# First kind of layer: the keys' squares summed ahead of scaling the queries, the differential outputs turned one group at a time, the gate's product kept apart from the powers

## The chip, the cores and the metric

The kernel runs on one core of one Trainium2 chip. The metric is the device time of one execution in microseconds. The engines are named as the profile has them: PE is TensorE (matmuls and transposes), PEld its weight loads, DVE is VectorE, ACT is ScalarE, POOL is GpSimd and SP is SyncE, which here only issues the loads of weights.

## The reference

The model has four layers on 256 rows of 1024 features: two of a first kind, then two of a second kind. The change touches only the first kind, and there only its mixing half:

```python
h = rms_norm(x, attn_norm_g[l])
rq, rk, rv, rg, dq, dk, dv = split(h @ w_in[l])            # 7 x 512 columns
ret = retention_bidir(rq, rk * 64 ** -0.5, rv, lg_f, lg_b) # 8 heads of 64
ret = rms_norm(ret, ret_norm_g[l]) * silu(rg)
dqn = rms_norm(dq, dq_norm_g[l]) * 64 ** -0.5              # 4 heads of 2 x 64
dkn = rms_norm(dk, dk_norm_g[l])
da  = diff_attention(dqn, dkn, dv, lam, slopes)            # 4 heads of 128
da  = rms_norm(da, diff_norm_g[l]) * (1 - lam_init)
x   = x + concatenate([ret, da]) @ w_out[l]
```

After that comes a gated feed-forward part (w_gate, w_up, w_down).

## The kernel before, in words

All matrix products of weights are float32 done in three passes. Weights are loaded by SyncE in slabs of 512 rows by 512 columns (128 partitions x 4 x 512) into a ring of four. ScalarE rounds a slab to its high half (`split_hi`, L1019), VectorE subtracts to get its low half (`split_lo`, L1512), and TensorE multiplies high by high, high by low and low by high (L492, L493, L494 for a whole slab, L509, L510, L511 for half of one). The splits run three slabs ahead of TensorE; a new load waits until the slab that lay in its place has been split.

Nothing is scheduled by a planner. Each engine has its own program, written out by hand in order, and waits on counting semaphores. The order within one engine's program is thus the order of its work, and a wait holds up all that is behind it on that engine.

A layer of the first kind projects `h` onto seven blocks of 512 columns: DQ, DK, DV, RQ, RK, RV, RG. While TensorE works on the later blocks, the attention of the earlier ones is put between its slabs by the generator `side()`. TensorE writes transposes and the heads' outputs into two turning banks, taken in turn. `turn_free` counts how many of them have been read out, so a piece of work can start only when the bank two before has been freed. `dve_ready` counts results of VectorE that are ready to be turned.

The steps that the change and the prediction touch are these.

* The scaled queries and keys of differential attention. ScalarE takes the projected block (`take_proj`, L1119) and squares it (`square_heads`, L1180). VectorE sums the squares over each head (`means`: the reduction is L1692, the mean L1561). GpSimd raises 16 columns to the power -0.5 (`root`, L2118), and VectorE multiplies (`norm_heads`, which calls `over_rms`, L1698). This is done for the queries (0) and for the keys (1). TensorE waits once for both, and turns the first two pairs of heads (`diff_pair`, transposes at L526).
* Retention. `ret_scores` (L632) makes the scores of a head, `retain` on VectorE (L1684) multiplies them by the decay, and `ret_values` (L649) makes the outputs of two heads in a turning bank. ScalarE copies these to `mixed1` (`take_outputs`, L1126) and squares a half of them, four heads, at a time (`square_outputs`, L1174). VectorE sums, GpSimd takes the power over 8 columns, and `ret_half` (L1698) multiplies the gated outputs by it.
* The gate. ScalarE takes the block RG through Silu (`take_proj(RG, 2, ACT.Silu)`, L1119, with a load of the activation table ahead of it). GpSimd multiplies the gate by the outputs, a half at a time (L2148).
* Turning `mixed1`. Eight tiles of 128 columns are turned in four groups of two: groups 2 and 3 are the differential outputs, 0 and 1 the retention outputs. ScalarE reads a turned group as its high half (`mixed_hi`, L1149) and VectorE as its low half (`mixed_lo`, L1541), which frees the bank. They are the left operands of w_out, whose four slabs are multiplied in half products of two tiles (`half_product`), so that TensorE can begin with the differential outputs while the retention outputs are still being made.

Before the change, `turn_mixed((2, 3))` (L665, called from `side()`) waits for `dve_ready` and turns both differential groups one behind the other, into both turning banks. ScalarE takes both high halves, then RG, then the outputs of heads 2 and 3. GpSimd does, for each half, the gate's product first (with a wait for its own result) and then the power. VectorE does a slab's split between each retention mean and the `ret_half` that belongs to it.

Of the kernel before, what the change touches and what calls it, by code (L numbers as in the profile page):

```python
# [24 lines left out]
ALU = mybir.AluOpType  # L25
# [113 lines left out]

STEPS_ACT1, STEPS_ACT2 = 4, 8  # L140
STEPS_DVE1, STEPS_DVE2 = 27, 86
STEPS_POOL1, STEPS_POOL2 = 2, 24
SMALL_LOADS = 5


# [39 lines left out]
def build(nc, t, out):  # L185
    with ExitStack() as ctx:
# [3 lines left out]
        def sem(name):  # L190
            return ctx.enter_context(nc.semaphore(name))
# [138 lines left out]
        decays_in = sem("decays_in")  # L330
        conv_in = sem("conv_in")
        outputs_in = sem("outputs_in")
        act_job = sem("act_job")
        conv_out = sem("conv_out")
        act_step = sem("act_step")
# [134 lines left out]
        def _(pe):  # L470
# [64 lines left out]
            def turn_model(src, groups, skip=0):  # L535

                for g in groups:
                    turn_group([(src[:, r, kt * P:(kt + 1) * P], (kt % 2) * SEQ + r * P)
                                for kt in (2 * g, 2 * g + 1) for r in range(R)], skip if g == groups[-1] else 0)
# [56 lines left out]
            for l in q.rounds(DEPTH, dict(slab=len(KTS1), blk=BLOCKS1, turn=TURNS1, scores=16, dve=9)):  # L596
# [62 lines left out]
                def ret_pair(j):  # L659
                    if j == 0:  # L660
                        read_out(projection[5])
                    group["ret", j] = turn_pair(lambda r: proj1[:, r, RQ + j * P:RQ + (j + 1) * P],
                                                lambda r: proj1[:, r, RK + j * P:RK + (j + 1) * P])

                def turn_mixed(groups):  # L665
                    pe.wait_ge(dve_ready, q.next("dve"))
                    turn_model(mixed1, groups)
                    return q.now("turn")

                def side():  # L670

                    pe.wait_ge(dve_ready, q.next("dve", 2))
                    diff_pair(0)
                    diff_pair(1)
                    yield
                    for h in range(DH):
                        diff_scores(h)
                        if h < 2:
                            diff_pair(h + 2)
                        else:  # L680
                            turn_combined(h - 2)
                        if h == 3:
                            diff_values(0)
                        yield
                    turn_combined(2)
                    diff_values(1)
                    ret_pair(0)
                    ret_pair(1)
                    yield
                    turn_combined(3)  # L690
                    diff_values(2)
                    ret_scores(0)
                    ret_scores(1)
                    yield
                    diff_values(3)
                    ret_values(0)
                    ret_scores(2)
                    ret_scores(3)
                    ret_pair(2)
                    yield  # L700
                    group["mixed"] = turn_mixed((2, 3))
                    ret_values(1)
                    ret_scores(4)
                    ret_scores(5)
                    ret_pair(3)
                    yield

# [10 lines left out]

                a = [open_block()]
                s = [take_slab()]  # L720
                pe.wait_ge(turn_free, group["mixed"] + 2)
                half_product(a[0], s[0], (0, 1), (0, 1), first=True)
                ret_values(2)
                ret_scores(6)
                ret_scores(7)
                turned_half = turn_mixed((0,))
                half_product(a[0], s[0], (2, 3), (2, 3)).then_inc(slab_used, 1)
                ret_values(3)
                s.append(take_slab())
# [2 lines left out]
                a.append(open_block())  # L732
                s.append(take_slab())
                half_product(a[1], s[2], (0, 1), (4, 5), first=True)
                turned_half = turn_mixed((1,))
                s.append(take_slab())
                half_product(a[1], s[3], (0, 1), (0, 1))
                pe.wait_ge(turn_free, turned_half + 2)
# [254 lines left out]
        def _(act):  # L993
# [110 lines left out]
            for l in q.rounds(DEPTH, per1):  # L1104
# [127 lines left out]
                decays((6, 7))  # L1232
                splits(1)
                mixed_hi(0, G_D)
                mixed_hi(2, G_D)
                take_proj(RG, 2, ACT.Silu)
                take_outputs(P)
                square_outputs(0, HALF)
                take_pair(3)
                splits(1)  # L1240
                take_outputs(2 * P)
# [253 lines left out]
        def _(dve):  # L1495
# [141 lines left out]
            loop4 = dict(slab=4, used=4, blk=2)  # L1637
            for l in q.rounds(DEPTH, dict(slab=len(KTS1), used=len(KTS1), blk=BLOCKS1, turn=TURNS1,
                                          turn_hi=4 + 4 + 11 + 4, squares=9, rstd=7, act_done=11, scores=16,
                                          decay=RH, probs=DH, step=STEPS_DVE1)):  # L1640
                ahead = iter(KTS1[AHEAD:] + KTS1[:AHEAD])

                def splits(n):
# [59 lines left out]
                def ret_half(c):  # L1703

                    root()
                    over_rms(mixed1[:, :, c * HALF:(c + 1) * HALF], proj1[:, :, RG + c * HALF:RG + (c + 1) * HALF],
                             S_OR + 8 * c, 4, HD).then_inc(dve_ready, 1)

# [23 lines left out]
                square_means(0)  # L1732
                splits(1)
                others(1)
                norm_heads(0)
                square_means(1)
                splits(1)
                norm_heads(1)
                splits(1)
# [20 lines left out]
                over_rms(v, v, S_PR, DH, DVD).then_inc(dve_ready, 1)  # L1760
                splits(1)
                mixed_lo(0, G_D)
                mixed_lo(2, G_D)
                others(2)
                q.next("turn", 3)
                retain((4, 5))
                means(S_O, sqo[:, :, 0:HALF], 4, HD)
                splits(1)
                ret_half(0)
                retain((6, 7))  # L1770
                mixed_lo(4, G_R)
                splits(1)
                q.next("turn")
                means(S_O + 8, sqo[:, :, HALF:NB], 4, HD)
                splits(1)
                ret_half(1)
                mixed_lo(6, G_R)
                added(0, l * 16 + 8)
                added(1, l * 16 + 8)
# [331 lines left out]
        def _(pool):  # L2111
# [17 lines left out]
            for l in q.rounds(DEPTH, dict(mean=7, outputs=2, decay=RH, blk=BLOCKS1, step=STEPS_POOL1)):  # L2129
                def diagonals(heads):  # L2130

                    for h in heads:
                        pool.wait_ge(decay_arg, q.next("decay"))
                        pool.tensor_tensor(decay[h][:, P:SEQ], decay[h][:, P:SEQ], decay[h][:, 3 * P:2 * SEQ],
                                           ALU.mult).then_inc(decay_ready, 1)

                root_x()
                root(stat[:, S_QR:S_QR + 16], stat[:, S_Q:S_Q + 16], 16)
                root(stat[:, S_QR + 16:S_QR + 32], stat[:, S_Q + 16:S_Q + 32], 16)
                diagonals(range(6))  # L2140
                root(stat[:, S_PR:S_PR + 8], stat[:, S_P:S_P + 8], 8)
                diagonals((6, 7))
                pool.wait_ge(acc_free, q.now("blk") + 7 + 2)
                for c in range(2):
                    pool.wait_ge(outputs_in, q.next("outputs"))
                    v = proj1[:, :, RG + c * HALF:RG + (c + 1) * HALF]
                    hold(pool)
                    step(pool.tensor_tensor(v, v, mixed1[:, :, c * HALF:(c + 1) * HALF], ALU.mult))  # L2148
                    at = 8 * c
                    root(stat[:, S_OR + at:S_OR + at + 8], stat[:, S_O + at:S_O + at + 8], 8)  # L2150
                root_x()
                q.next("blk", BLOCKS1)
            for l in q.rounds(DEPTH, dict(mean=4, blk=BLOCKS2, step=STEPS_POOL2)):
# [69 lines left out]
```

## Time and profile before

| | |
|---|---|
| runs | 1497.16, 1498.7 and 1499.43 us, median 1498.7 |
| the profiled execution: time, span | 1496.12 us, 1494.3 us |
| mean granted clock of TensorE | 0.995 of full speed |
| PE busy | 1446.4 us, 97% of the span |
| DVE busy | 942.6 us, 63% |
| ACT busy | 783.3 us, 52% |
| POOL busy | 105.1 us, 7% |
| split to the low half, L1512 | 251 instructions, 2187 ns mean |
| split to the high half, L1019 | 251 instructions, 1825 ns mean |
| power, L2118 | 23 instructions, 2475 ns mean |

The span runs from the first to the last instruction of the profiled execution; its time is 1.8 us more. The part of the span before about 322 us is layer one of the first kind, that from there to about 645 us is layer two, and the second kind follows. The granted clock is given as a share of TensorE's full 2.4 GHz. A matmul's end is modelled, and the starts are exact, so distances between starts are the better measure of TensorE.

### The profile page before, as it was taken

Reading aid. Unit: us, or ns where it says so; the run is one execution under the profiler, and the core shown is the slowest. Engines: PE = TensorE matmul, PEld = TensorE weight load, DVE = VectorE, ACT = ScalarE, POOL = GpSimd, SP = SyncE. Lnnn points to the kernel's source line nnn. Section 1 sums busy time; section 2 is a strip of 40 time slices with the busy share of each in tenths; the row PEclk is TensorE's granted clock in tenths of the full one; section 3 lists DMA queues with packets and bytes.
Section 4 is the critical chain, followed back from the end, with each engine's and each line's share of the span. In section 5 each row is a group of like instructions: output and inputs, shape, how many; then the busy total and the mean of one; then the engine's idle time right before and its main releaser. Section 6 shows DMA issues by size and latency. Waiting matters only on the chain.

```text
span 1494.3 us, 21705 instructions
## 1 busy us (share of the span) xinstructions
PE 1446.4 (97%) x7095; PEld 1203.2 (81%) x7095; DVE 942.6 (63%) x1120; ACT 783.3 (52%) x1012; POOL 105.1 (7%) x111
## 2 busy tenths in 40 slices
PE   5999999999999999999999999999999999999997
PEld 4787888888778888887888888888778888888885
DVE  5565655445755655445678878764456788787544
ACT  5574644345664444445666546544366765465442
POOL 0213000001212000000220000000002200000000
PEclk9999999999999999999999999999999999999998
DMA  7543555464433655555344566555553545666541
GB/s 278 194 140 115 172 194 193 144 205 163 154 128 111 228 190 175 169 198 179 114 164 148 190 225 197 179 192 192 172 180 113 177 151 175 224 197 196 190 149 43
DMA packets 174070, 257.74 MB, mean 172 GB/s; under 512 B 8765, under 2 KB 91919, under 8 KB 173839
## 3 DMA queue, kind: packets, MB, share of 16 engines
q1 hardware_dynamic: 170432, 249.95, 50.6%
q10 hardware_dynamic: 3535, 6.51, 1.4%
q8 instruction: 52, 0.85, 0.2%
q14 instruction: 51, 0.42, 0.1%
HBM read 255.39 MB, written 1.05 MB: 172 GB/s over the span
## 4 chain that ended last, share of the span: by engine, by line
PE 53%; issue 40%; POOL 3%; DVE 2%; ACT 1%; DMA 1%; ACTq 0%; DVEq 0%; POOLq 0%
PE bank L492 13%; PE bank L494 13%; PE bank L493 13%; PE bank L954 4%; PE bank L526 3%; POOL stat L2118 2%; PE bank L953 2%; PE bank L649 1%; PE bank L632 1%; PE bank L606 1%; DMA crows<-in_conv_rows 1%; PE bank L509 1%; PE bank L510 1%; PE bank L511 0%; PE bank L623 0%
## 5 line engine op out<-in xcount | busy, mean ns | idle before, releaser
L1512 DVE TENSOR_TENSOR w_lo<-w_raw,w_hi 128x2048 fp32r<-128x2048 f32 (+1 forms) x251 | 547.6, 2187 | 221.3 <-ACT w_hi L1019 218.5
L1019 ACT CAST w_hi<-w_raw 128x2048 fp32r<-128x2048 f32 (+1 forms) x251 | 455.9, 1825 | 226.1 <-PE bank L494 204.4
L492 PE MATMUL bank<-w_hi,hT 128*128 128x512 f32 (+1 forms) x1056 | 419.1, 397 | 7.7 <-DVE w_lo L1512 6.1
L494 PE MATMUL bank<-w_hi,hT 128*128 128x512 f32 (+1 forms) x1056 | 411.8, 390 | 0.0
L493 PE MATMUL bank<-w_lo,hT 128*128 128x512 f32 (+1 forms) x1056 | 411.1, 389 | 0.0
L492 PEld LDWEIGHTS bank<-w_hi,hT 128*128 128x128 f32 x1056 | 199.0, 188 | 48.4 <-DVE w_lo L1512 6.5
L494 PEld LDWEIGHTS bank<-w_hi,hT 128*128 128x128 f32 x1056 | 198.8, 188 | 41.5
L493 PEld LDWEIGHTS bank<-w_lo,hT 128*128 128x128 f32 x1056 | 199.2, 189 | 38.1
L954 PE MATMUL bank<-hT,w_hi 128*128 128x512 f32 x512 | 178.2, 396 | 0.4 <-DVE sum L2061 0.4
L2118 POOL TENSOR_TENSOR stat<-stat,cst 128x2 f32<-128x2 f32 (+3 forms) x23 | 56.9, 2475 | 1155.6 <-DVE stat L1561 1015.3
L953 PE MATMUL bank<-hT,w_lo 128*128 128x256 f32 x448 | 125.2, 279 | 0.0
L954 PEld LDWEIGHTS bank<-hT,w_hi 128*128 128x128 f32 x512 | 94.4, 188 | 21.4 <-issue 1.3
L492 PE MATMUL bank<-w_hi,hid2T_hi 128*128 128x512 f32 x256 | 99.8, 390 | 0.0
L494 PE MATMUL bank<-w_hi,hid2T_lo 128*128 128x512 f32 x256 | 99.7, 389 | 0.0
L493 PE MATMUL bank<-w_lo,hid2T_hi 128*128 128x512 f32 x256 | 99.6, 389 | 0.0
L953 PEld LDWEIGHTS bank<-hT,w_lo 128*128 128x128 f32 x448 | 84.4, 188 | 1.3
L492 PE MATMUL bank<-w_hi,hid1T_hi 128*128 128x512 f32 x176 | 69.1, 392 | 0.0
L494 PE MATMUL bank<-w_hi,hid1T_lo 128*128 128x512 f32 x176 | 68.6, 390 | 0.0
L493 PE MATMUL bank<-w_lo,hid1T_hi 128*128 128x512 f32 x176 | 68.5, 389 | 0.0
L1541 DVE SCALAR_TENSOR_TENSOR hT<-bank,gcols,hT 128x256 fp32r<-128x256 f32 (+1 forms) x76 | 34.2, 506 | 48.7 <-ACT hT L1049 41.4
L1042 ACT CAST hid1T_hi<-bank 128x512 f32 (+1 forms) x22 | 12.9, 586 | 90.3 <-PE bank L526 90.3
L1462 ACT COPY cross<-bank 128x256 f32<-128x256 f32 x64 | 20.8, 378 | 70.8 <-PE bank L954 70.8
(261 smaller groups left out, 1637.5 us busy)
## 6 DMA issues: line engine op xcount, KB each, us to landing
w_raw<-in_w_gate SPq DMA_DIRECT2D x108, 512.0 KB, 3.9
w_raw<-in_w_up SPq DMA_DIRECT2D x108, 512.0 KB, 4.5
w_raw<-in_w_down SPq DMA_DIRECT2D x104, 512.0 KB, 4.4
w_raw<-in_w_in SPq DMA_DIRECT2D x88, 512.0 KB, 4.3
w_raw<-in_w_out SPq DMA_DIRECT2D x16, 512.0 KB, 4.1
w_raw<-in_w_branch SPq DMA_DIRECT2D x32, 256.0 KB, 3.0
w_raw<-in_w_o SPq DMA_DIRECT2D x16, 512.0 KB, 4.6
bgate<-in_b_gate ACTq DMA_DIRECT2D x16, 256.0 KB, 3.3
```

What stands on the lines that cost most here:

```text
L492: pe.matmul(o, hi[:, kt, rows_of(r)], w_hi[:, s, j, 0:cols], start=begin, stop=False)
L493: pe.matmul(o, hi[:, kt, rows_of(r)], w_lo[:, s, j, 0:cols], start=False, stop=False)
L494: mm = pe.matmul(o, lo[:, kt, rows_of(r)], w_hi[:, s, j, 0:cols], start=False, stop=end)
L509: pe.matmul(a[r][:, :], hT_hi[:, kt, rows_of(r)], w_hi[:, s, j, :], start=begin, stop=False)
L526: tr = pe.transpose(b[0:m, col:col + n], src, ident[0:n, 0:n])
L953: pe.matmul(o[:, 0:SEQ], lo[:, kt, cols], hT_hi[:, kt, :], start=False, stop=False)
L954: mm = pe.matmul(o[:, :], hi[:, kt, cols], hT[:, :, kt, :], start=kt == 0, stop=kt == KT - 1)
L1019: act.copy(w_hi[:, s, 0:kts, :], w_raw[:, s, 0:kts, :]).then_inc(hi_ready, 1)
L1462: ins = act.copy(cross2[:, n, :], a[n][:, SEQ:2 * SEQ])
L1512: dve.tensor_tensor(w_lo[:, s, 0:kts, :], w_raw[:, s, 0:kts, :], w_hi[:, s, 0:kts, :].bitcast(F32), ALU.subtract).then_inc(lo_ready, 1)
L1541: return dve.scalar_tensor_tensor(lo, src, gain, hi.bitcast(F32), ALU.mult, ALU.subtract)
L2118: pool.tensor_tensor(dst, src, half[:, 0:n], ALU.pow).then_inc(rstd_ready, 1)
```

## The change

On TensorE the wait on `dve_ready` moves out of `turn_mixed`, which now turns one group. Group 2 is turned where both were, group 3 behind the values of heads 2 and 3 and the scores of heads 4 and 5, and the second half product of the first slab gets a wait for group 3.

On ScalarE the outputs of heads 2 and 3 are taken and squared ahead of RG, and the high half of group 3 is taken behind RG.

On VectorE the keys' squares are summed ahead of scaling the queries. The low half of group 3 moves behind the retention mean of the first four heads. In both halves of the retention outputs the slab's split moves from ahead of `ret_half` to behind it, and `ret_half` waits for a new semaphore, `gated`.

On GpSimd the gate's product signals `gated` instead of being waited for by GpSimd itself, and the order becomes power 0, product 0, product 1, power 1 where it was product 0, power 0, product 1, power 1.

```diff
@@ counts of self-waits, and the semaphore
-STEPS_POOL1, STEPS_POOL2 = 2, 24
+STEPS_POOL1, STEPS_POOL2 = 0, 24
+        gated = sem("gated")
@@ TensorE
-                def turn_mixed(groups):
-                    pe.wait_ge(dve_ready, q.next("dve"))
-                    turn_model(mixed1, groups)
+                def turn_mixed(g):
+                    turn_model(mixed1, (g,))
                     return q.now("turn")
...
-                    group["mixed"] = turn_mixed((2, 3))
+                    pe.wait_ge(dve_ready, q.next("dve"))
+                    group["mixed", 0] = turn_mixed(2)
                     ret_values(1)
                     ret_scores(4)
                     ret_scores(5)
+                    group["mixed", 1] = turn_mixed(3)
                     ret_pair(3)
...
-                pe.wait_ge(turn_free, group["mixed"] + 2)
+                pe.wait_ge(turn_free, group["mixed", 0] + 2)
                 half_product(a[0], s[0], (0, 1), (0, 1), first=True)
                 ret_values(2)
                 ret_scores(6)
                 ret_scores(7)
-                turned_half = turn_mixed((0,))
+                pe.wait_ge(dve_ready, q.next("dve"))
+                turned_half = turn_mixed(0)
+                pe.wait_ge(turn_free, group["mixed", 1] + 2)
                 half_product(a[0], s[0], (2, 3), (2, 3)).then_inc(slab_used, 1)
...
-                turned_half = turn_mixed((1,))
+                pe.wait_ge(dve_ready, q.next("dve"))
+                turned_half = turn_mixed(1)
@@ ScalarE
                 mixed_hi(0, G_D)
-                mixed_hi(2, G_D)
-                take_proj(RG, 2, ACT.Silu)
                 take_outputs(P)
                 square_outputs(0, HALF)
+                take_proj(RG, 2, ACT.Silu)
+                mixed_hi(2, G_D)
                 take_pair(3)
@@ VectorE
                 def ret_half(c):
 
                     root()
+                    dve.wait_ge(gated, q.next("gated"))
...
                 square_means(0)
                 splits(1)
                 others(1)
+                square_means(1)
                 norm_heads(0)
-                square_means(1)
                 splits(1)
                 norm_heads(1)
...
                 mixed_lo(0, G_D)
-                mixed_lo(2, G_D)
                 others(2)
-                q.next("turn", 3)
+                q.next("turn")
                 retain((4, 5))
                 means(S_O, sqo[:, :, 0:HALF], 4, HD)
-                splits(1)
+                mixed_lo(2, G_D)
+                q.next("turn", 2)
                 ret_half(0)
+                splits(1)
                 retain((6, 7))
                 mixed_lo(4, G_R)
                 splits(1)
                 q.next("turn")
                 means(S_O + 8, sqo[:, :, HALF:NB], 4, HD)
-                splits(1)
                 ret_half(1)
+                splits(1)
                 mixed_lo(6, G_R)
@@ GpSimd
-                pool.wait_ge(acc_free, q.now("blk") + 7 + 2)
-                for c in range(2):
+                def gate_half(c):
+                    v = proj1[:, :, RG + c * HALF:RG + (c + 1) * HALF]
                     pool.wait_ge(outputs_in, q.next("outputs"))
-                    v = proj1[:, :, RG + c * HALF:RG + (c + 1) * HALF]
                     hold(pool)
-                    step(pool.tensor_tensor(v, v, mixed1[:, :, c * HALF:(c + 1) * HALF], ALU.mult))
+                    pool.tensor_tensor(v, v, mixed1[:, :, c * HALF:(c + 1) * HALF], ALU.mult).then_inc(gated, 1)
+
+                def root_half(c):
                     at = 8 * c
                     root(stat[:, S_OR + at:S_OR + at + 8], stat[:, S_O + at:S_O + at + 8], 8)
+
+                root_half(0)
+                pool.wait_ge(acc_free, q.now("blk") + 7 + 2)
+                gate_half(0)
+                gate_half(1)
+                root_half(1)
```

## Rows read from the trace of the kernel before

**Rows 1.** Waits of TensorE over the span: total us, times, longest us.
```profile
PE bank L649 <- DVE hT L1541: 3.0, 2, 1.5
```

**Rows 2.** Timeline of TensorE, 55 to 59 us: start us, us, instruction, [idle before <-releaser].
```profile
55.38 0.39 PE L494 MATMUL bank<-w_hi,hT 128*128 128x512 f32 x1
57.37 1.09 PE L526 MATMUL bank<-cst,proj 128*128 128x128 f32 x8 [1.60 <-DVE proj L1698]
58.21 0.47 PE L492 MATMUL bank<-w_hi,hT 128*128 128x512 f32 x1
```

**Rows 3.** Timeline of VectorE, 49 to 58 us.
```profile
49.53 1.22 DVE L1692 TENSOR_REDUCE stat<-proj 128x16 f32<-128x1024 f32 x1
...
50.87 2.28 DVE L1512 TENSOR_TENSOR w_lo<-w_raw,w_hi 128x2048 fp32r<-128x2048 f32 x1
55.94 1.29 DVE L1698 TENSOR_TENSOR proj<-proj,stat 128x512 f32<-128x512 f32 x2 [2.79 <-POOL stat L2118]
```

**Rows 4.** Timeline of ScalarE, the keys' square.
```profile
46.22 1.06 ACT L1180 ACTIVATE proj<-proj 128x1024 f32<-128x1024 f32 x1
```

**Rows 5.** Timeline of GpSimd, 50 to 166 us.
```profile
51.03 4.87 POOL L2118 TENSOR_TENSOR stat<-stat,cst 128x16 f32<-128x16 f32 x1 [2.75 <-DVE stat L1561]
...
113.42 1.64 POOL L2118 TENSOR_TENSOR stat<-stat,cst 128x8 f32<-128x8 f32 x1 [26.09 <-DVE stat L1561]
...
124.27 1.28 POOL L2148 TENSOR_TENSOR proj<-proj,mixed 128x512 f32<-128x512 f32 x1 [7.29 <-ACTq L1173]
127.05 3.63 POOL L2118 TENSOR_TENSOR stat<-stat,cst 128x8 f32<-128x8 f32 x1 [1.50 <-DVE stat L1561]
...
162.74 2.70 POOL L2118 TENSOR_TENSOR stat<-stat,cst 128x2 f32<-128x2 f32 x1 [20.18 <-DVE stat L1561]
```

**Rows 6.** Timeline of VectorE, splits that ran beside powers.
```profile
126.90 2.29 DVE L1512 TENSOR_TENSOR w_lo<-w_raw,w_hi 128x2048 fp32r<-128x2048 f32 x1
...
162.59 4.49 DVE L1512 TENSOR_TENSOR w_lo<-w_raw,w_hi 128x2048 fp32r<-128x2048 f32 x2
```

**Rows 7.** Timeline of TensorE, layer one, 119 to 144 us.
```profile
119.04 1.03 PE L526 MATMUL bank<-cst,mixed 128*128 128x128 f32 x8
121.57 1.99 PE L649 MATMUL bank<-proj,ret_p 128*128 128x64 f32 x16 [1.50 <-DVE hT L1541]
123.49 1.14 PE L632 MATMUL bank<-qkT 64*128 64x256 f32 x8
124.57 0.66 PE L526 MATMUL bank<-cst,proj 128*128 128x128 f32 x4
...
127.83 1.89 PE L649 MATMUL bank<-proj,ret_p 128*128 128x64 f32 x16
...
131.53 0.66 PE L526 MATMUL bank<-cst,mixed 128*128 128x128 f32 x4 [0.74 <-DVE mixed L1698]
...
134.79 1.89 PE L649 MATMUL bank<-proj,ret_p 128*128 128x64 f32 x16
...
143.41 0.66 PE L526 MATMUL bank<-cst,mixed 128*128 128x128 f32 x4 [1.18 <-DVE mixed L1698]
```

**Rows 8.** Timeline of ScalarE, 119 to 125 us.
```profile
119.84 1.26 ACT L1149 ACTIVATE hT<-bank,gcols 128x512 fp32r<-128x512 f32 x2 [2.02 <-PE bank L526]
121.12 1.28 ACT L1119 ACT_TABLE_LOAD   x1
122.42 1.26 ACT L1119 ACTIVATE proj<-bank,stat 128x512 f32<-128x512 f32 x2
...
124.17 0.63 ACT L1174 ACTIVATE sqo<-mixed 128x512 f32<-128x512 f32 x1
```

**Rows 9.** Timeline of TensorE, layer two.
```profile
378.52 1.09 PE L526 MATMUL bank<-cst,proj 128*128 128x128 f32 x8 [1.59 <-DVE proj L1698]
...
465.30 0.66 PE L526 MATMUL bank<-cst,mixed 128*128 128x128 f32 x4 [1.18 <-DVE mixed L1698]
```

**Rows 10.** Busy us by window: PE, PEld, DVE, ACT, POOL, then granted clock, DMA.
```profile
445.00:446.00 1.00, 1.00 (x8) 0.65 (x4) 0.00 (x0) 0.81 (x2) 0.59 (x1) 0.50 0.02 7
```

More of the change, by code:

```diff
@@ L1639, in _ @@
                                           turn_hi=4 + 4 + 11 + 4, squares=9, rstd=7, act_done=11, scores=16,
-                                          decay=RH, probs=DH, step=STEPS_DVE1)):
+                                          decay=RH, probs=DH, gated=2, step=STEPS_DVE1)):
                 ahead = iter(KTS1[AHEAD:] + KTS1[:AHEAD])
@@ L1762, in _ @@
                 mixed_lo(0, G_D)
-                mixed_lo(2, G_D)
                 others(2)
-                q.next("turn", 3)
+                q.next("turn")
                 retain((4, 5))
                 means(S_O, sqo[:, :, 0:HALF], 4, HD)
+                mixed_lo(2, G_D)
+                q.next("turn", 2)
+                ret_half(0)
                 splits(1)
-                ret_half(0)
                 retain((6, 7))
@@ L1774, in _ @@
                 means(S_O + 8, sqo[:, :, HALF:NB], 4, HD)
+                ret_half(1)
                 splits(1)
-                ret_half(1)
                 mixed_lo(6, G_R)
```

## The prediction

> **What bounds the kernel now.** I read the page first: TensorE is busy for 97% of the span and no other engine for more than 63%, so only idle time of TensorE, or a lower clock on it, can be won back. Then the list of who TensorE waited for. Nearly all of its waits in the two layers of the first kind that this change touches are on VectorE, and they stand at four places, which the timeline of TensorE shows one by one. A: before the first diff pair is turned, 1.60 us for the scaled keys [rows 2]. B: before the retention values of heads 2 and 3, 1.50 us until a turning bank comes free, once in each layer, 3.0 us in all [rows 1, 7]. C: before the first pair of gated retention outputs is turned, 0.74 us. D: before the second pair, 1.18 us [rows 7]. In layer two A and D repeat (1.59 and 1.18) [rows 9], B repeats [rows 1], and C is missing, because TensorE arrived later there: its granted clock was 0.50 just behind B [rows 10], half of the 2.4 GHz that it has elsewhere. The distance from A to D is 86.04 us in layer one (57.37 to 143.41) and 86.78 in layer two (378.52 to 465.30) [rows 2, 7, 9], so that stretch cost 0.74 us net.
>
> Next I ask what makes VectorE late at A, C and D. It is each time GpSimd's power (L2118). Eight columns took 1.64 us at 113.42, but 3.63 us at 127.05, and the difference is VectorE's split of a slab (L1512), which ran from 126.90 to 129.19: the power ended 1.49 us behind it. Sixteen columns at 51.03 took 4.87 us and ended 2.75 us behind the split of 50.87. Two columns at 162.74 ended at 165.44, 0.56 us behind the first of two splits and in the middle of the second [rows 3, 5, 6]. So a power stands still while VectorE subtracts two SBUF tiles, and goes on when that one instruction ends; its own time is 1.64 us for 8 columns and about 2.8 for 16.
>
> **A: keys' squares ahead of scaling the queries.** ScalarE's square of the keys ends at 46.22 + 1.06 = 47.28 [rows 4]. VectorE reduces at 47.3 rather than at 49.53; the power can start 1.50 us behind the reduction (49.53 to 51.03) [rows 3, 5], at 48.8. The queries' scaling then runs on VectorE from 48.7 to 50.0 (1.29 us in two halves [rows 3]) and the split behind it to 52.2. Both read two SBUF tiles, so what the power does between them isn't shown by any row; the nearest is the two-column power, which was let in between two such instructions. I take that: in at 49.4, done at 52.1. The other end is a power held behind all three, 52.2 + 2.75 = 54.95. The keys' scaling leads TensorE by 1.43 us (55.94 to 57.37) [rows 2, 3]. That gives 53.6 or 56.4. TensorE itself could start at 55.61, a matmul's 0.23 behind the last at 55.38 [rows 2]. Gain: 57.37 - 55.61 = 1.76 us a layer, with 1.0 as the lower end. The added wait (VectorE now waits for ScalarE's second square before it scales the queries) costs nothing: TensorE takes both scalings with one wait, and the first power ends at 48.3 in any case.
>
> **B: one group at a time.** Eight transposes took 0.84 us (57.37 to 58.21) [rows 2], so four take 0.42. In the frame of layer one before: group 2 at 119.04, the values at 119.46 in the other bank with no wait, scores 1.92 later at 121.38, group 3 1.08 later at 122.46, the pair at 122.88, and a pair with its half product is 3.26 (124.57 to 127.83) [rows 7], so the next values could start at 126.14. Group 3 finds its bank free: the low half of group 2 is out by about 121.5, as before. But a new wait takes B's place. The next values need the bank of group 3, and ScalarE now reads it last: values end at 119.46 + 1.99 = 121.45, the square starts 0.61 behind that (123.56 to 124.17), 0.63 for it, 1.28 for the table, 1.26 for the gate's projection, and 1.73 from the high half's start to TensorE (119.84 to 121.57) [rows 7, 8]: 126.97. So 1.50 becomes 0.83, at the next values.
>
> **C and D: gate apart from the powers, splits behind the gated scaling.** From 126.97, values and scores take 131.53 - 0.74 - 127.83 = 2.96 [rows 7]: TensorE is at C at 129.93. What it needs there: the power starts 3.56 us behind the scores of heads 4 and 5 (123.49 to 127.05) [rows 5, 7], so at 124.94. No split runs beside it now, 1.64: 126.58. The gate's product, 1.28 [rows 5], is behind it rather than ahead: 127.9. The scaling reaches TensorE 0.85 us on (130.68 to 131.53): 128.7, over 1 us early. That margin also covers the low half of group 3, which VectorE takes from PSUM beside this power, should it hold the power up. C is gone. TensorE is at the last values at 129.93 + 3.26 = 133.19. From there to D it has work for 8.62 - 1.18 = 7.44 us (134.79 to 143.41), where the chain through copy, square, power and scaling took the whole 8.62 [rows 7]. Without the split beside the power it is 8.62 - 1.99 = 6.63: under 7.44. D is gone, at 133.19 + 7.44 = 140.63 against 143.41, a gain of 2.78. The second gate product runs beside VectorE's reduction, which has one SBUF input.
>
> The two splits that move wait some 2 us longer. What stands behind them: the decayed scores of heads 6 and 7, done at about 132.4 for values at 133.2 (the thinnest margin, 0.8 us), and the loads of the slabs four further on, where a slab keeps TensorE for twice 3.26 - 0.42 = 2.84 us [rows 7], so over 20 us on. I take nothing for both; with that margin gone it would be under 1 us a layer. The semaphore and the two dropped self-waits cost nothing, since GpSimd is 7% busy.
>
> **The sum.** Layer one 1.76 + 2.78 = 4.54. Layer two the same, and 0.74 if the clock stays up, since the idle time that stood ahead of its fall is gone: 5.28. Together 9.8 us. The profiled execution had 1494.3 us of span in 1496.12 and becomes 1484.5 in 1486.3; the median of the runs shown is 2.6 us above it, and I take the 9.8 off that: 1498.7 - 9.8 = **1488.9**.
>
> **A rule against the trace.** The trace shows the splits at 162.59 taking 4.49 us for two, each its usual time, with a power let in between them [rows 5, 6]: the power did not stop the second one. The Trainium skill, in "SBUF — State Buffer", section "Who interferes with whom", says that VectorE with two SBUF inputs and GpSimd share one pair of ports as a lock held for the whole instruction, and that the other fully blocks. The trace agrees on who makes the power wait and not on the reverse; by the rule the sum would be that of the first rival.
>
> **Rivals.** First, GpSimd's power, once in, holds VectorE up as well. At A it would be in from 49.4 to 52.1, the second half of the queries' scaling (0.65) and the split (2.28) follow, 55.0, and TensorE starts at 56.45: A gains 0.9 instead of 1.76. 1498.7 - 8.1 = 1490.6. For it speaks only that 16 columns are more than the 2 of the row. Chance 0.17.
> Second, 3.63 and 4.87 us are the powers' own times and the splits only happen to be there. A still gains 1.76 (48.8 + 4.87 + 1.43 = 55.1). At C it is 124.94 + 3.63 + 1.28 + 0.85 = 130.7, then 3.26 and 8.62: D at 142.6, a gain of 0.8. Two layers at 2.6, with the low clock kept: 1493.5. The 1.64 us speaks against it. Chance 0.10.
> Third, on the other side: both together, the power for the keys held back until 52.2 and then 4.87 us long. It ends at 57.1, TensorE starts A at 58.5, 1.15 us later than now, and with 0.8 back at D each layer loses 0.35: 1499.4. It decides once that power ends over 0.8 us behind its present 55.9. Chance 0.03.
> Fourth, the clock: if it falls in the dense run of small matmuls at B, a layer loses up to 1.6 us (layer two lost 0.74 and the 0.8 that C would have cost). Both layers: 1498.7 - 9.1 + 3.2 = 1492.8. Chance 0.08.
>
> **How the numbers follow.** The likeliest case has 0.62 and gives 1488.9, by itself 1486.5 to 1490. All idle time gone and none new would be 1486; another stretch of low clock, in the second kind, can move by a microsecond or two with everything that comes earlier, so the low end is 1485.5. The high end takes in the first, the second and the fourth rival: 1494. A measurement of this kernel can tell about 0.2%, 3 us. Faster than 1495.7 are all cases but the third and accidents: 0.95. Within 3 us 0.04, slower 0.01.
>
> **What would show it.** In the profile after: TensorE's wait for the scaled keys gone; that for the gated outputs gone at C and D; its wait for a turning bank moved to the values of heads 4 and 5, near 0.8 us; the powers of 8 columns all at 1.64 us and the keys' at 3.3 (let in) or 6 (held); clock 1.00 near 445. I am wrong if the keys' power ends later than 54.2, if the 8 columns still take 3.6, or if a wait at the last values appears.

## The result and the profile after

The changed kernel took 1485.16 us in the median of four runs (1483.96 to 1486.15), the kernel before 1498.46 in the same session. The medians are 13.3 us apart; the ratio of the two kernels is put at 0.9917, with a 95% interval of 0.9905 to 0.993, which is 12.4 us less, and the 12.4 is used below. The forecast was 1488.9, in a range of 1485.5 to 1494. The profiled execution took 1486.15 us with a span of 1484.3, against 1496.12 and 1494.3 before: 10.0 us less.

TensorE's timeline in layer one (start us, us, instruction, [idle before <-releaser]; a line number is 1 higher than before, and from ScalarE's part on 5 to 7 higher):

```profile
55.35 1.03 PE L527 MATMUL bank<-cst,proj 128*128 128x128 f32 x8
...
116.94 0.60 PE L527 MATMUL bank<-cst,mixed 128*128 128x128 f32 x4
117.37 1.90 PE L650 MATMUL bank<-proj,ret_p 128*128 128x64 f32 x16
119.19 1.14 PE L633 MATMUL bank<-qkT 64*128 64x256 f32 x8
120.27 0.66 PE L527 MATMUL bank<-cst,mixed 128*128 128x128 f32 x4
120.76 0.60 PE L527 MATMUL bank<-cst,proj 128*128 128x128 f32 x4
...
124.57 1.99 PE L650 MATMUL bank<-proj,ret_p 128*128 128x64 f32 x16 [0.46 <-DVE hT L1546]
126.50 1.14 PE L633 MATMUL bank<-qkT 64*128 64x256 f32 x8
127.57 0.66 PE L527 MATMUL bank<-cst,mixed 128*128 128x128 f32 x4
...
130.81 1.89 PE L650 MATMUL bank<-proj,ret_p 128*128 128x64 f32 x16
...
138.09 0.60 PE L527 MATMUL bank<-cst,mixed 128*128 128x128 f32 x4
```

Where [rows 2, 7] have four waits (1.60, 1.50, 0.74, 1.18) there is one, 0.46 us, and it stands ahead of the values of heads 4 and 5. From the first differential transpose to the second retention group (B to D below) TensorE takes 21.15 us (116.94 to 138.09) instead of 24.37. The list of TensorE's waits after, for the whole span (total us, times, longest), has this in place of [rows 1] and nothing from the gated outputs or the scaled keys:

```profile
PE bank L650 <- DVE hT L1546: 0.9, 2, 0.5
```

GpSimd's timeline after:

```profile
48.56 3.30 POOL L2125 TENSOR_TENSOR stat<-stat,cst 128x16 f32<-128x16 f32 x1 [0.54 <-DVE stat L1566]
...
122.74 1.64 POOL L2125 TENSOR_TENSOR stat<-stat,cst 128x8 f32<-128x8 f32 x1 [7.87 <-DVE stat L1566]
124.34 1.27 POOL L2154 TENSOR_TENSOR proj<-proj,mixed 128x512 f32<-128x512 f32 x1
...
134.95 1.64 POOL L2125 TENSOR_TENSOR stat<-stat,cst 128x8 f32<-128x8 f32 x1 [0.25 <-DVE stat L1566]
```

The keys' power took 4.87 us in [rows 5] and takes 3.30; both powers of the retention outputs take 1.64 instead of 3.63. VectorE's timeline around the keys' power:

```profile
47.05 1.22 DVE L1697 TENSOR_REDUCE stat<-proj 128x16 f32<-128x1024 f32 x1 [1.80 <-ACT proj L1185]
48.31 0.17 DVE L1566 TENSOR_SCALAR stat<-stat 128x16 f32<-128x16 f32 x1
48.41 1.32 DVE L1703 TENSOR_TENSOR proj<-proj,stat 128x512 f32<-128x512 f32 x2
49.65 2.28 DVE L1517 TENSOR_TENSOR w_lo<-w_raw,w_hi 128x2048 fp32r<-128x2048 f32 x1
51.89 1.29 DVE L1703 TENSOR_TENSOR proj<-proj,stat 128x512 f32<-128x512 f32 x2
```

The power was done at 51.86. Its own time of about 2.75 us (what it had left behind the split in [rows 3, 5]) puts its real start near 49.1, and that is where the first half of the scaling ended; the profile has no row for that moment, so this start is worked out. The second half and the whole split ran in that time at their usual lengths: from there on neither side held the other up.

In layer two A starts at 371.51 and D at 454.29, where [rows 9] have 378.52 and 465.30:

```profile
454.29 0.60 PE L527 MATMUL bank<-cst,mixed 128*128 128x128 f32 x4
```

The low clock of [rows 10] is gone there, but the profiled execution has a new stretch of it later (busy us of PE, PEld, DVE, ACT, POOL, then granted clock, DMA share, GB/s):

```profile
444.00:446.00 2.00, 2.00 (x12) 1.70 (x11) 2.00 (x5) 0.69 (x1) 0.00 (x0) 1.00 0.00 0
...
1146.00:1148.00 2.00, 2.00 (x9) 2.00 (x8) 2.00 (x3) 0.51 (x1) 0.00 (x0) 0.57 0.12 43
```

The 10.0 us of the profiled executions add up from the starts of A and D in both: up to A of layer one 2.02 less (1.76 of it at A, the rest in the first microseconds of the program), to D 3.30, to A of layer two 1.69, to D 4.00 (with the clock), and from there to the end it takes 1.01 more (1030.0 against 1029.0). That is the stretch near 1146, where the granted clock was 0.57 over 2 us and the kernel before had full clock: a second profiled execution of the changed kernel (after_again, below) has no such stretch and takes 1028.8 us from D to the end.

### The profile page after: what moved, and what is told of

It reads as the page before. It is cut to its first block, busy times and chain, and to the rows that moved or that the text cites. A ratio compares the mean times of both kernels' runs of the same rounds, so it can differ in the third digit from the quotient of the medians.

```text
span 1484.3 us, 21707 instructions
## 1 busy us (share of the span) xinstructions
PE 1445.0 (97%) x7095; PEld 1203.6 (81%) x7095; DVE 942.6 (64%) x1120; ACT 782.8 (53%) x1012; POOL 93.9 (6%) x111
## 4 chain that ended last, share of the span: by engine, by line
PE 71%; issue 23%; DVE 2%; POOL 1%; ACT 1%; DMA 1%; ACTq 0%; DVEq 0%; POOLq 0%
PE bank L493 18%; PE bank L495 18%; PE bank L494 18%; PE bank L959 4%; PE bank L527 4%; PE bank L958 2%; PE bank L650 1%; PE bank L510 1%; PE bank L512 1%; PE bank L511 1%; PE bank L607 1%; PE bank L633 1%; ACT w_hi L1024 1%; DMA crows<-in_conv_rows 1%; PE bank L624 0%
## 5 line engine op out<-in xcount | busy, mean ns | idle before, releaser
L2125 POOL TENSOR_TENSOR stat<-stat,cst 128x2 f32<-128x2 f32 (+3 forms) x23 | 45.8, 1991 | 1163.8 <-DVE stat L1566 1023.6
```

Source lines behind the costliest of these rows:

```text
L2125: pool.tensor_tensor(dst, src, half[:, 0:n], ALU.pow).then_inc(rstd_ready, 1)
```

## The experiments

The theory was the prediction's: a power on GpSimd stands still while VectorE runs one instruction with two SBUF inputs, and each wait of TensorE goes by what ends last in its chain. I tried three of the parts alone on the kernel before (the keys, the splits, the turning), and took parts out of the changed one; GpSimd's new order was tried only there.

**The keys' squares alone.** In the kernel before:

```diff
-                norm_heads(0)
                 square_means(1)
+                norm_heads(0)
```

> The kernel before with one edit: the keys' squares are summed ahead of scaling the queries. Theory (the power is let in between two instructions of VectorE with two SBUF inputs): the keys' power starts near 48.8 us, takes 3.3 us, and TensorE turns the first pair with no wait, 1.76 us earlier in each layer: 3.5 us less than before. Rival (the power, once in, holds VectorE up, or is held back by all of it): the power ends near 55 us or the split behind the scaling takes over 4 us, and each layer gains 0.9 to 1.0: 1.9 us less.

Measured: 1493.39 us in the median against 1497.22, ratio 0.9975 (0.9965 to 0.9985), 3.7 us less. Its power and the start of A (timelines of GpSimd and TensorE):

```profile
49.14 3.30 POOL L2118 TENSOR_TENSOR stat<-stat,cst 128x16 f32<-128x16 f32 x1 [0.54 <-DVE stat L1561]
```
```profile
55.92 1.04 PE L526 MATMUL bank<-cst,proj 128*128 128x128 f32 x8
```

No wait at A. The matmul before it started at 55.69, 0.23 earlier, so the 1.76 us are whole. B, C and D keep 1.50, 0.74 and 1.18 in layer one. The split behind the scaling took 2.28 us beside the power, in this execution too. The first rival of the prediction falls here.

**The splits alone.** In the kernel before:

```diff
-                splits(1)
                 ret_half(0)
+                splits(1)
...
-                splits(1)
                 ret_half(1)
+                splits(1)
```

> The kernel before with two splits moved from ahead of the gated scaling to behind it, nothing else. Theory (the split stops the power beside it): both powers of 8 columns over the retention outputs fall from 3.63 to 1.64 us, the waits at C and D are gone, the wait at B stays 1.50. From the first transpose of the differential outputs to D layer one takes 22.2 us instead of 24.37; both layers together 3.5 us less than before. Rival (3.63 us is the power's own time): the powers stay, C and D stay, 24.4 us and no change in time.

Measured: 1493.53 us against 1497.22, ratio 0.9976 (0.9966 to 0.9986), 3.6 us less. GpSimd's power at C, then TensorE from B to D in layer two:

```profile
127.30 1.64 POOL L2118 TENSOR_TENSOR stat<-stat,cst 128x8 f32<-128x8 f32 x1 [2.46 <-DVE stat L1561]
```
```profile
439.89 1.03 PE L526 MATMUL bank<-cst,mixed 128*128 128x128 f32 x8
442.42 1.99 PE L649 MATMUL bank<-proj,ret_p 128*128 128x64 f32 x16 [1.50 <-DVE hT L1541]
...
462.11 0.60 PE L526 MATMUL bank<-cst,mixed 128*128 128x128 f32 x4
```

B to D is 22.22 us, as the theory had it, with 1.50 left at B and nothing at C and D. In layer one of this execution the clock fell behind B and the same stretch took 25.38. A window there:

```profile
122.00:124.00 2.00, 2.00 (x11) 1.72 (x12) 0.00 (x0) 1.27 (x3) 0.43 (x1) 0.50 0.30 104
```

**The turning alone.** In the kernel before, TensorE's and ScalarE's part of the diff, and on VectorE:

```diff
                 mixed_lo(0, G_D)
-                mixed_lo(2, G_D)
                 others(2)
-                q.next("turn", 3)
+                q.next("turn")
                 retain((4, 5))
                 means(S_O, sqo[:, :, 0:HALF], 4, HD)
+                mixed_lo(2, G_D)
+                q.next("turn", 2)
                 splits(1)
                 ret_half(0)
```

> The kernel before with only the turning of one group at a time (TensorE's order, ScalarE's order, the low half of group 3 behind the retention mean); splits, gate and keys as before. Theory (what the turning saves at B is taken back at C while the power is long): the wait of 1.50 us at B is gone, one of 0.46 us stands at the next values, and at C a split of VectorE starts just ahead of the power, so that it takes 3.6 us and TensorE waits 1.3 to 1.5 us there; 1.18 at D stays. From the first transpose of the differential outputs to D 24.0 us in place of 24.37, 0.8 us in all at the same mean clock. Rival (each part's gain stands by itself): 1.1 us a layer, 2.2 us in all. On the clock: if its falls come from the idle time at B, the mean clock is 0.995 or more in nearly all runs, where the kernel before has 0.991 to 0.994 in about half; if any idle time there will do, it is as before.

Measured: 1495.0 us against 1498.52, ratio 0.9981 (0.997 to 0.9991), 2.8 us less. Most of that is the clock: all eleven runs have a mean of 0.995 or 0.996, where 11 of the 15 of the kernel before have less, and those of 0.996 start at 1493.32 us against 1493.84. TensorE in layer one:

```profile
118.08 0.60 PE L526 MATMUL bank<-cst,mixed 128*128 128x128 f32 x4
...
125.72 1.99 PE L649 MATMUL bank<-proj,ret_p 128*128 128x64 f32 x16 [0.46 <-DVE hT L1545]
...
130.26 0.66 PE L526 MATMUL bank<-cst,mixed 128*128 128x128 f32 x4 [1.48 <-DVE mixed L1702]
...
142.13 0.66 PE L526 MATMUL bank<-cst,mixed 128*128 128x128 f32 x4 [1.20 <-DVE mixed L1702]
```

B to D is 24.05 us. So the wait of 1.50 was not won but pushed on: 0.46 at the next values and 1.48 at C, where it had been 0.74. What stands at C is the power (timelines of GpSimd and VectorE):

```profile
125.93 3.48 POOL L2123 TENSOR_TENSOR stat<-stat,cst 128x8 f32<-128x8 f32 x1 [0.16 <-POOL proj L2153]
```
```profile
125.51 2.41 DVE L1516 TENSOR_TENSOR w_lo<-w_raw,w_hi 128x2048 fp32r<-128x2048 f32 x1
```

It ended 1.49 us behind the split's end at 127.92, the same 1.49 as in [rows 5, 6]. The rival by which each part's gain stands by itself is out.

**Both groups at once in the changed kernel.** The turning undone, all else left: `turn_mixed(2)` and `turn_mixed(3)` one behind the other, ScalarE's and VectorE's order of that step as before.

> The changed kernel with both differential groups turned one behind the other again, and ScalarE's and VectorE's order of that step as before. Theory: the wait of 1.50 us at B is back and that of 0.46 us at the next values is gone; C and D stay free, since the powers stay short. From the first transpose of the differential outputs to D layer one takes 22.2 us against 21.15, so 2.1 us more for both layers at the same clock. If the idle time at B is also what lets the clock fall there, some runs show a lower mean clock (0.993 or 0.994 instead of 0.995 to 0.996) and the median is 3 to 4 us higher. Rival (turning one group at a time is worth nothing, the splits did it all): the same time.

Measured: 1487.47 us against 1496.13, ratio 0.9939 (0.9922 to 0.9956). That is 2.3 to 2.6 us above the changed kernel's medians of 1485.16 and 1484.9 in two other sessions; 2.1 was expected at the same clock.

```profile
116.93 1.03 PE L527 MATMUL bank<-cst,mixed 128*128 128x128 f32 x8
119.47 1.99 PE L650 MATMUL bank<-proj,ret_p 128*128 128x64 f32 x16 [1.50 <-DVE hT L1546]
...
139.19 0.60 PE L527 MATMUL bank<-cst,mixed 128*128 128x128 f32 x4
```

B to D is 22.26 us, 1.11 more than 21.15. The turning is thus worth 0.32 us a layer while the powers are long (24.37 to 24.05) and 1.11 once they are short.

**The second split put back** ahead of `ret_half(1)`.

> The changed kernel with the second of the two splits put back ahead of the gated scaling. Theory: that power is 3.63 us again, and the wait at D comes back as 134.95 + 3.63 + 0.04 + 0.85 = 139.5 against 138.1: 1.4 us a layer, 2.8 us in all, the first power stays 1.64. Rival (the new order on GpSimd or the turning brought D's gain): D stays without a wait and the time stays.

Measured: 1488.89 us against 1497.22, ratio 0.9946 (0.9929 to 0.9963), 3.7 to 4.0 us above the changed kernel's medians in other sessions, where 2.8 was expected. GpSimd's second retention power and TensorE at D:

```profile
135.39 3.64 POOL L2125 TENSOR_TENSOR stat<-stat,cst 128x8 f32<-128x8 f32 x1 [0.24 <-DVE stat L1566]
```
```profile
139.97 0.66 PE L527 MATMUL bank<-cst,mixed 128*128 128x128 f32 x4 [1.28 <-DVE mixed L1703]
```

D started 22.59 us behind B, 1.44 later than in the changed kernel; 1.4 was expected.

**The first split put back** right behind `means(S_O, ...)`.

> The changed kernel with the first of the two splits put back right behind the first retention mean. Theory: the power beside it takes 3.63 us, but C's wait doesn't come back, because the low half of group 3 is now 2.3 us later on VectorE and the wait at the values of heads 4 and 5 grows from 0.46 to about 1.6 us; both layers lose 1.2 us each. Rival (the first split's place doesn't matter): the same 21.15 us from the first differential transpose to D.

Measured in a single run of 1491.6 us: GpSimd's power took 3.63 us, and TensorE's wait was where the theory had it, with no wait at C.

```profile
125.63 2.79 PE L650 MATMUL bank<-proj,ret_p 128*128 128x64 f32 x16 [1.57 <-DVE hT L1546]
```

B to D took 4.28 us more in layer one and 2.68 in layer two (25.43 and 23.83), not the 1.2 expected, since behind this wait the clock fell in both layers:

```profile
128.00:130.00 2.00, 2.00 (x10) 1.44 (x10) 0.37 (x2) 0.37 (x1) 0.00 (x0) 0.50 0.93 326
...
448.00:450.00 2.00, 2.00 (x10) 1.33 (x9) 0.72 (x2) 0.64 (x2) 0.00 (x0) 0.50 1.05 371
```

**The gate's product first again** in the changed kernel: `gate_half(0)`, `root_half(0)`, `gate_half(1)`, `root_half(1)`.

> The changed kernel with the old order on GpSimd: the gate's product ahead of the first power. Theory (the order is worth nothing once the power is short): the product starts when the gate is out at about 123.1, ends at 124.4, the power ends at 126.0 where product and power ended at 125.6, so the gated scaling is 0.4 us later, TensorE could be served at 127.0, and it gets there at 127.6: no wait at C, the same time. Rival (C went because the gate is kept apart): the wait at C comes back with 0.7 us a layer or more, 1.5 us in all.

Measured: 1484.13 us against 1497.22, ratio 0.9915 (0.9898 to 0.9932). B to D is 21.17 us and there is no wait at C:

```profile
123.05 1.28 POOL L2154 TENSOR_TENSOR proj<-proj,mixed 128x512 f32<-128x512 f32 x1 [8.46 <-ACT proj L1124]
124.29 1.64 POOL L2125 TENSOR_TENSOR stat<-stat,cst 128x8 f32<-128x8 f32 x1
```

The new order on GpSimd does not shorten anything once the power is short. The splits alone say the same from the other side: with the old order they take B to D to 22.22 us, and both groups at once, with the new order, to 22.26.

**An instruction with one SBUF input beside the power.** In the changed kernel, behind `means(S_O + 8, ...)`, with a result that nothing uses:

```diff
+                dve.tensor_reduce(stat[:, S_Z:S_Z + 4],
+                                  cst[:, 0:2048].rearrange("p (n c) -> p n c", n=4), AX.X, ALU.max)
```

> The changed kernel with a reduction of 2048 columns of one SBUF tile added on VectorE just behind the second retention mean, where the split was before; its result isn't used. Theory (only an instruction of VectorE with two SBUF inputs stops the power): the reduction takes about 2.3 us beside the power, which stays 1.64 us, and TensorE waits at D for 0.1 us at most. Rival (any long instruction of VectorE on SBUF stops it): the power takes 3.6 us, and D gets a wait of over 1 us.

Measured in a single run of 1484.58 us (timelines of VectorE and GpSimd):

```profile
134.69 2.28 DVE L1782 TENSOR_REDUCE stat<-cst 128x4 f32<-128x2048 f32 x1
```
```profile
134.86 1.64 POOL L2126 TENSOR_TENSOR stat<-stat,cst 128x8 f32<-128x8 f32 x1 [0.24 <-DVE stat L1566]
```

The reduction is as long as the split and stands at the same place, and the power keeps its 1.64 us in both layers; TensorE did not wait at D. Nor is it the second input as such. In the kernel before, the power of 113.42 in [rows 5] took 1.64 us while `retain` multiplied scores in PSUM (bank) by decays in SBUF, four times:

```profile
113.36 1.42 DVE L1684 SCALAR_TENSOR_TENSOR ret_p<-bank,proj 128x256 f32<-128x256 f32 x4
```

In these runs what stops the power is an instruction with two inputs in SBUF.

**The high half of group 3 ahead of the gate's block.** The one wait left is ScalarE's order, so in the changed kernel:

```diff
                 square_outputs(0, HALF)
-                take_proj(RG, 2, ACT.Silu)
                 mixed_hi(2, G_D)
+                take_proj(RG, 2, ACT.Silu)
```

> The changed kernel with ScalarE taking the high half of group 3 ahead of the gate's block instead of behind it. Theory (the new wait of 0.46 us at the values of heads 4 and 5 is ScalarE's table load and gate ahead of that high half): the wait is gone, the gate is out 0.7 us later and its product still ends near 125.7, so C and D stay free: 0.55 us less in each layer, 1.1 us in all. Rival (the gate's product becomes what C waits for): the wait moves to C and nothing is won.

Measured: 1483.53 us against 1496.13, ratio 0.9908 (0.9892 to 0.9925). TensorE in layer one:

```profile
115.88 0.60 PE L527 MATMUL bank<-cst,mixed 128*128 128x128 f32 x4
...
122.90 1.89 PE L650 MATMUL bank<-proj,ret_p 128*128 128x64 f32 x16
...
136.33 0.60 PE L527 MATMUL bank<-cst,mixed 128*128 128x128 f32 x4
```

No wait from A to D in either layer, and B to D is 20.45 us, 0.70 less than in the changed kernel. The intervals of the two ratios overlap, so both were run again side by side.

> The changed kernel itself once more, on the chip of the next one. At the same mean clock 10.0 us less than the kernel before; mean clock 0.995 to 0.996 in nearly all runs.

> The version with the high half of group 3 ahead of the gate's block, beside the changed kernel on one chip. Theory: no wait of TensorE from A to D in either layer, and 1.1 to 1.4 us less than the changed kernel at the same mean clock. Rival: the difference seen before was the clock's, and the two are the same.

Measured: the changed kernel 1484.9 us (1484.45 to 1486.61, five runs), this version 1482.64 (1481.94 to 1483.42, four runs): no run of one lies among those of the other. It is 2.3 us faster, 1.4 of which are the two times 0.70 (where the rest comes from stays open), and it beats both kernels.

**The clock in more runs.** Every run lists its mean granted clock. The kernel before has 0.994 or less in 30 of its 52 runs beside the experiments (1496.1 to 1499.9 us) and 0.995 or 0.996 in the others (1493.8 to 1496.3 us). The same count for the others: the keys alone 6 of 10, the splits alone 6 of 10, the turning alone 0 of 11, the changed kernel 1 of 9. The mean counts every fall of the program, not only those behind B, and one short fall can hide in it: the profiled execution of the kernel before has 0.995 with one near 445. Since both groups at once had 0 of 4 in spite of its wait at B, it was run again.

> The changed kernel with both differential groups turned at once, for its mean clock in more runs. If the idle 1.50 us at B is enough to let the clock fall there, about half of the runs have a mean clock of 0.991 to 0.994 and the median is near 1489; if it needs the other waits (A, C, D) around it, nearly all runs have 0.995 or more and lie between 1486.5 and 1488.

Measured: 1487.57 us (1486.76 to 1488.99), 0 of 6.

## Why the prediction was right, and where it was off

The time fell as forecast, by more than was said: 12.4 us for 9.8. On the time of before that was shown, the ratio gives 0.9917 x 1498.7 = 1486.3, inside the range of 1485.5 to 1494; the session's own median of 1485.16 is 0.3 us below its low end. The mechanism was right at every step; that the profiled execution met its sum so closely (1486.15 us against 1486.3) was in part luck, as the last point shows. By the steps:

* **A: right.** 1.76 us a layer, to the hundredth, by the case it took: the power was let in behind the first half of the scaling, near 49.1, and was done at 51.86. The other end (55 us, by the first rival) is refuted by the changed kernel's own trace and by the part alone.
* **B: right in kind, the new wait sized too high.** It appeared at the values of heads 4 and 5, with 0.46 us and not 0.83. Three terms were long. The values ahead of ScalarE's chain take 1.90 us and not 1.99, which was the row behind a wait. ScalarE's gate block starts 1.16 us ahead of the high half behind it (121.81 to 122.97) and not 1.26, since the rows of two instructions overlap. The way from that start to TensorE is 1.60 us (122.97 to 124.57) and not 1.73. In [rows 8] the high half stood first of two, and I took that distance as it was. ScalarE's rows:

```profile
120.52 1.28 ACT L1124 ACT_TABLE_LOAD   x1
121.81 1.27 ACT L1124 ACTIVATE proj<-bank,stat 128x512 f32<-128x512 f32 x2
122.97 0.69 ACT L1154 ACTIVATE hT<-bank,gcols 128x512 fp32r<-128x512 f32 x1
```

* **C and D: right.** No wait at either, powers of 1.64 us. From the values of heads 6 and 7 to D it is 7.28 us (130.81 to 138.09) and not 7.44: I had taken the profile's idle time of 1.18 off 8.62, and that leaves out the part of the gap that the modelled end of a matmul covers. B to D gained 3.22 us against 2.78: the wait that was sized too high makes 0.37 of the difference, the work up to D 0.16, and small terms elsewhere take 0.09 back.
* **The splits moved back** cost nothing, as said. No wait stands at the last values.
* **Layer two: right.** A to D gained 4.00 us where layer one gained 3.30, so the clock gave 0.70; 0.74 was forecast.
* **The sum: right in total, with two terms off.** The work was put at 4.54 us a layer, 9.1 in all. At equal clock the profiled executions give 1.76 at A, 1.69 up to A of layer two, and 3.30 from A to D in each layer: 10.05. The missing 1.0 us is that of B to D. It doesn't show in the 10.0 us between the two profiled executions (9.8 forecast), because the new stretch of low clock near 1146 cost about as much. The other term is the last. I took 9.8 off the median of before as if its runs differed from the profiled one by chance, but they differ by the clock: 30 of 52 runs of before have a mean of 0.994 or less, its profiled execution had 0.995, and with the change it was 1 of 9. At a mean clock of 0.996 the lowest runs of before are near 1494.1 (1493.84 to 1494.23 over four sessions) and those of the changed kernel near 1484.4 (1483.96 to 1484.9), a difference of 9.7 us. The rest of the 12.4 us goes with the clock; the prediction gave it 0.74. The fourth rival had the clock falling more often at B, and it falls less.

The rivals: the first (a power holds VectorE up) and the second (3.63 us is the power's own) are out by the runs above, and the third needs the second. The parts' gains add up for A only. Alone, A is worth 1.76 us a layer at equal clock, the splits 2.15 (24.37 to 22.22) and the turning 0.32, and splits and turning together 3.22, more than their sum (2.47): with a long power at C, time saved ahead of it is lost at it.

The prediction weighed the page "SBUF — State Buffer" of the Trainium skill, section "Who interferes with whom". Its sentence that `tensor_reduce` on this chip never contends agrees with the 1.64 us beside the reduction of 2.28. The prediction took from it that a GpSimd instruction which is in holds VectorE up for its whole length (that section of the Trainium skill writes "for the whole instruction" of VectorE's two-port modes). The powers don't show that: the split from 49.65 ran its usual 2.28 us beside one. GpSimd's products come nearer to it. A split started at 114.48, 0.40 us before a product of decays ended, and took 2.55 us, 0.27 more than usual:

```profile
113.19 1.69 POOL L2141 TENSOR_TENSOR decay<-decay 128x128 f32<-128x128 f32 x2 [0.23 <-ACT decay L1161]
```
```profile
114.48 2.55 DVE L1517 TENSOR_TENSOR w_lo<-w_raw,w_hi 128x2048 fp32r<-128x2048 f32 x1
```

**What stays open** is why the clock falls. All five falls that the profiled executions show in these two layers came behind a wait of 1.5 us that matmuls of 64 columns follow: one each in the kernel before, the keys alone and the splits alone, two with the first split put back. But there are falls elsewhere too. In the second kind TensorE waits twice for 1.75 us for VectorE (L876 in the kernel before, L881 in the changed one); behind the first of these the clock fell in 13 of the 14 profiled executions, behind the second in 8, the one near 1146 among them. So the same wait, in the same code, is followed by a fall in one execution and not in the next, and the prediction's remark that TensorE has its full clock elsewhere was not so: the kernel before falls near 745 as well. (Every profiled execution also spends its last 8 to 11 us at half clock; these are left out here.)

Nor is the wait at B enough by itself. With both groups at once it is the only one left: its two profiled executions have no fall behind it, and none of ten runs had a low mean. The keys alone (waits at B, C and D) and the splits alone (at A and B) have a low mean as often as the kernel before. What has to come to the wait was not found, and that a low mean comes from B in the runs without a profile is an inference.

## What to carry to other kernels

When GpSimd's small instructions are on a critical chain, look at what VectorE runs beside them: here an instruction with two SBUF inputs stopped them and one with a single SBUF input didn't, and moving it behind the result cost nothing, since its own deadline was far. Take the parts of a reordering together and walk the chain to the next wait, since a wait removed upstream of a longer chain only moves. And compare kernels at the same mean clock before ascribing a difference to the schedule.

## What the runs showed of the hardware that was not expected

A power of 16 columns that waits for VectorE is let in between two halves of one scaling, 0.65 us apart, and then neither it nor the following instructions of VectorE with two SBUF inputs are slower (3.30 us in all, of which 2.75 are its own by [rows 3, 5]). In every profiled execution, changed or not, a free power of 8 columns takes 1.64 us, and one that a split stopped ends 1.5 us behind it.

The granted clock falls to half for stretches of some 3.5 to 7 us, behind waits of TensorE of only 1.5 to 1.75 us, and the same wait is followed by a fall in some executions only. For the changed kernel that is worth a microsecond or so: its profiled execution with a fall near 1146 took 1486.15 us, the one without 1484.9.
